# A chunkwise recurrence on TensorE: two key operands side by side in one stationary operand, one product for the turned rows of both, and the state step over 128 rows

## The reference

```python
def step(S, inp):
    r_t, w_t, k_t, v_t, kk_t, a_t = inp
    sa = jnp.einsum('bhvk,bhk->bhv', S, -kk_t)
    S = (S * w_t[:, :, None, :] + sa[..., None] * (kk_t * a_t)[:, :, None, :]
         + v_t[..., None] * k_t[:, :, None, :])
    return S, jnp.einsum('bhvk,bhk->bhv', S, r_t)
```

## Time and profile before

| | us |
|---|---|
| median of 3 executions | 2036.55 (2035.19 to 2040.31) |
| profiled execution, own time | 2034.68 |
| its span in the trace | 2032.9 |
| TensorE busy | 2001.4 |
| line 956 busy, each layer | 70.32 |
| one turn of the recurrence loop | 14.64 |

### The profile page before, as it was taken

The page is one execution under the profiler, slowest core; times in us unless marked ns, Lnnn a source line. Parts: engine busy times, 40 slices in busy tenths (PEclk is TensorE's granted clock), DMA queues, the critical chain, the costliest instruction groups (busy, mean ns, idle before and its releaser), DMA issues.

```text
span 2032.9 us, 36044 instructions
## 1 busy us (share of the span) xinstructions
PE 2001.4 (98%) x15296; PEld 1761.3 (87%) x15296; DVE 1496.4 (74%) x1311; ACT 1199.0 (59%) x1076; POOL 53.6 (3%) x36
## 2 busy tenths in 40 slices
PE   8999999999999999999999999999999999999998
PEld 6978999999998888899988888888888888888886
DVE  6656356765455766438578898888889889898896
ACT  5454453543343545445467777777777777777675
POOL 0003100000000001200000000000000000000000
PEclk9999999999999999999999999999999999999999
DMA  7432035444442322105459899898998989899895
GB/s 239 172 111 97 4 133 201 166 166 172 187 162 106 142 106 86 41 27 225 179 224 380 344 358 373 323 372 336 369 367 335 373 334 364 349 359 372 326 376 199
DMA packets 75038, 485.60 MB, mean 239 GB/s; under 512 B 13480, under 2 KB 14632, under 8 KB 17192
## 3 DMA queue, kind: packets, MB, share of 16 engines
q1 hardware_dynamic: 73816, 481.93, 61.3%
q10 hardware_dynamic: 1104, 1.92, 0.3%
HBM read 482.08 MB, written 1.74 MB: 238 GB/s over the span
## 4 chain that ended last, share of the span: by engine, by line
PE 92%; DVE 4%; ACT 2%; DMA 1%; issue 1%; POOL 0%; ACTq 0%; SPq 0%; DVEq 0%
PE PS L576 26%; PE PS L578 25%; PE PS L577 25%; PE PS L956 6%; DVE area L1910 1%; PE PS L1282 1%; PE PS L1291 1%; DVE WL L1910 1%; ACT WH L1442 1%; PE PS L914 1%; DMA ring<-in_weights 1%; PE PS L731 1%; DVE YEL L2515 0%; PE PS L1358 0%; PE PS L847 0%
## 5 line engine op out<-in xcount | busy, mean ns | idle before, releaser
L1910 DVE TENSOR_TENSOR WL<-ring,WH 128x2048 fp32r<-128x2048 f32 x410 | 934.4, 2290 | 218.0 <-ACT WH L1442 109.3
L1442 ACT ACTIVATE WH<-ring 128x2048 fp32r<-128x2048 f32 x336 | 643.1, 1916 | 158.5 <-PE PS L578 149.0
L576 PE MATMUL PS<-WH,XGH 128*128 128x512 f32 x896 | 353.7, 395 | 0.2 <-DVE XGL L1910 0.2
L578 PE MATMUL PS<-WL,XGH 128*128 128x512 f32 x896 | 349.7, 390 | 0.0
L577 PE MATMUL PS<-WH,XGL 128*128 128x512 f32 x896 | 349.1, 390 | 0.0
L578 PE MATMUL PS<-XL,WH 128*128 128x272 f32 (+1 forms) x704 | 202.5, 288 | 0.0
L1434 ACT ACTIVATE WH<-ring 128x2048 fp32r<-128x2048 f32 x74 | 141.3, 1910 | 102.0 <-PE PS L578 102.0
L578 PEld LDWEIGHTS PS<-WL,XGH 128*128 128x128 f32 x896 | 168.1, 188 | 35.8
L576 PEld LDWEIGHTS PS<-WH,XGH 128*128 128x128 f32 x896 | 168.3, 188 | 34.6 <-DVE WL L1910 0.5
L577 PEld LDWEIGHTS PS<-WH,XGL 128*128 128x128 f32 x896 | 168.4, 188 | 33.5
L576 PE MATMUL PS<-WH,HTH 128*128 128x512 f32 x448 | 176.7, 394 | 0.6
(11 more groups left out here) (350 smaller groups left out, 3432.7 us busy)
## 6 DMA issues: line engine op xcount, KB each, us to landing
ring<-in_experts SPq DMA_DIRECT2D x336, 1024.0 KB, 6.6
ring<-in_weights SPq DMA_DIRECT2D x114, 1024.0 KB, 6.9
ring<-in_weights SPq DMA_DIRECT2D x4, 576.0 KB, 4.4
ring<-in_weights SPq DMA_DIRECT2D x4, 512.0 KB, 4.0
cst<-in_consts SPq DMA_DIRECT2D x1, 1731.0 KB, 7.4
hT<-in_stream ACTq DMA_DIRECT2D x2, 544.0 KB, 7.0
out<-area SPq DMA_DIRECT2D x4, 256.0 KB, 2.0
bias_line<-lin SPq DMA_DIRECT2D x1, 672.0 KB
```

Source lines behind the costliest of these rows:

```text
L576: pe.matmul(o, lh, rh, start=first, stop=False, skip_group_check=True)
L578: return pe.matmul(o, lh, rl, start=False, stop=last, skip_group_check=True)
L1442: act.activation(WH[(BASE + j + 1) % 3][:, :], ring[b][:, 2048 * (j % 2):2048 * (j % 2) + 2048], ACT.Copy).then_inc(S("w_hi"), 1)
L1910: tt = lambda o, a_, b_, op: dve.tensor_tensor(o, a_, b_, op)
```

## The change

POOL writes AI and K of one chunk side by side into a buffer of its own (`double_keys`, four copies of 64 rows by 256, one after the other), so that they are one stationary operand of 128 columns. `products_m` multiplies it with RK in 8 matmuls on 64\*128 tiles; before these were two wide sets. `turn_rows` turns both with 8 matmuls on 64\*128 tiles and V with 8 on 64\*64; before these were three narrow sets, that of V in `products_b`. `state_step` is 8 matmuls on 128\*64 tiles instead of 16 on 64\*64. Solution and turned V now stand in one buffer UV, one in the upper and one in the lower 64 rows, so `copied_solution` becomes two ACT copies, and `copied_rows` four. DVE's `open_turned` has two half operations and stands behind `power(c - 1, 5)`; `open_rows` reads PSUM itself. `right_side` and `outputs_known` are split in a part with V and one with the state. POOL masks with four operations instead of two. In all the program has 7921 matmuls instead of 8145. Helpers that only pass an operand (`both` with `swapped`, `of_head`) and two merged semaphores are left out of the diff.

```diff
+        def doubled_keys(c):
+            home = area1[:, 8064 + 512 * c:8064 + 512 * c + 512] if c < 2 else slots_area[:, 512 * (c % 2):512 * (c % 2) + 512]
+            return home.rearrange("p (a x b) -> p a x b", a=4, x=2)
...
+                def products_m(c):
+                    cc = columns(c)
                     if c >= 2:
                         pe.wait_ge(S("r_yc"), nth(l, c - 2))
-                    both(2 + s_, 0, KK[:, :, cc], lambda r, p: AI[r, p, cc])
-                    both(2 + s_, 256, V[:, :, cc], lambda r, p: C("stack")[r, :]).then_inc(S("r_n"), 1)
-                    both(0, 0, AI[:, :, cc], lambda r, p: RK[r, :, p, cc], 2 * CH).then_inc(S("r_b"), 1)
-                def products_h(c):
-                    cc = columns(c)
-                    if c >= 2:
                         pe.wait_ge(S("r_state"), earlier(l, c - 2, lambda q: q < NCH - 1) + 1)
-                    both(1, 0, K[:, :, cc], lambda r, p: RK[r, :, p, cc], 2 * CH).then_inc(S("r_h"), 1)
+                    pe.wait_ge(S("keys_doubled"), nth(l, c))
+                    for p in range(4):
+                        for g in range(2):
+                            ins = pe.matmul(PS[:, g, 2 * CH * p:2 * CH * p + 2 * CH], doubled_keys(c)[heads[g], p, :, :].rearrange("p x b -> p (x b)"), RK[heads[g], :, p, cc],
+                                            start=True, stop=True, skip_group_check=True)
...
-                    cc = columns(c)
-                    pe.wait_ge(S("r_bc"), nth(l, c))
-                    both(0, 0, AI[:, :, cc], lambda r, p: C("stack")[r, :])
-                    both(0, 256, K[:, :, cc], lambda r, p: C("stack")[r, :]).then_inc(S("r_t"), 1)
+                    pe.wait_ge(S("r_hc"), nth(l, c))
+                    for p in range(4):
+                        for g in range(2):
+                            pe.matmul(PS[:, g, CH * p:CH * p + CH], doubled_keys(c)[heads[g], p, :, :].rearrange("p x b -> p (x b)"), C("stack")[heads[g], :],
+                                      start=True, stop=True, skip_group_check=True)
+                    for p in range(4):
+                        for g in range(2):
+                            ins = pe.matmul(PS[heads[1 - g], g, 256 + CH * p:256 + CH * p + CH], V[heads[g], p, columns(c)], C("stack")[heads[g], :],
+                                            start=True, stop=True, skip_group_check=True)
+                    ins.then_inc(S("r_t"), 1)
...
-                        both(1, 0, BHT[s_][:, 0], lambda r, p: Ust[r, p, :], first=True)
-                        both(1, 0, BHT[s_][:, 1], lambda r, p: NV[s_][r, 1, p, :], first=False).then_inc(S("r_s"), 1)
...
+                    both(1, 0, lambda g, p: BHT[s_][:, g, p, :], lambda g, p: UV[s_][:, g, p, :]).then_inc(S("r_s"), 1)
...
-                products_h(0)
-                products_b(0)
-                gate_steps(3)
+                products_n(0)
+                gate_steps(1)
+                products_m(0)
+                gate_steps(2)
                 turn_rows(0)
                 gate_steps(3)
                 level_product(0, 1)
-                pe.wait_ge(S("r_tc"), nth(l, 0))
-                products_b(1)
...
-                        products_b(c)
                         level_product(c - 1, 4)
-                        products_h(c)
+                        products_m(c)
                         level_update(c - 1, 4)
                         level_product(c - 1, 5)
-                        level_product(c, 1)
                         turn_rows(c)
                         level_update(c - 1, 5)
-                        right_side(c - 1)
+                        level_product(c, 1)
+                        right_values(c - 1)
+                    outputs_values(c - 1)
+                    if c > 1:
+                        right_state(c - 1)
                     level_update(c, 1)
                     solve(c - 1)
+                    if c > 1:
+                        outputs_state(c - 1)
                     level_product(c, 2)
                     state_step(c - 1)
+                    outputs_solved(c - 1)
                     level_update(c, 2)
-                    outputs_known(c - 1)
                     level_product(c, 3)
-                    outputs_solved(c - 1)
+                    if c + 1 < NCH:
+                        products_n(c + 1)
                     level_update(c, 3)
                 level_product(NCH - 1, 4)
-                right_side(NCH - 1)
+                right_values(NCH - 1)
                 pe.wait_ge(S("x_lo"), 5 * l + 1)
                 pe.wait_ge(S("w_lo"), g_first + 1)
...
+                def copied_m(c):
                     act.wait_ge(S("r_b"), nth(l, c))
-                    act.activation(BA[s_][:, :, :, :].rearrange("p a x b -> p (a x b)"), PS[:, 0, :], ACT.Copy).then_inc(S("r_bc"), 1)
...
-                    act.activation(BHT[s_][:, :, :, :].rearrange("p x a b -> p (x a b)"), PS[:, 0, :], ACT.Copy).then_inc(S("r_tc"), 1)
+                    for g in (1, 0):
+                        act.activation(BHT[s_][:, g, :, :], PS[:, g, 0:256].rearrange("p (a b) -> p a b", a=4), ACT.Copy)
+                        o = heads[1 - g]
+                        act.activation(UV[s_][o, g, :, :], PS[o, g, 256:512].rearrange("p (a b) -> p a b", a=4), ACT.Copy).then_inc(S("r_tc"), 1)
...
-                    act.activation(Ust[:, :, :], rows4(0), ACT.Copy).then_inc(S("r_uc"), 1)
+                    for g, o in enumerate(heads):
+                        ins = act.activation(UV[c % 2][o, g, :, :], PS[o, 1, 0:256].rearrange("p (a b) -> p a b", a=4), ACT.Copy)
+                    ins.then_inc(S("r_uc"), 1)
...
+                def double_keys(c):
+                    cc = slice(c * CH, (c + 1) * CH)
+                    o = doubled_keys(c)
+                    link(pool, pool.tensor_copy(o[0:HD, :, 0, :], AI[0:HD, :, cc]), "pool_chain")
+                    link(pool, pool.tensor_copy(o[0:HD, :, 1, :], K[0:HD, :, cc]), "pool_chain")
+                    link(pool, pool.tensor_copy(o[HD:P, :, 0, :], K[HD:P, :, cc]), "pool_chain")
+                    pool.tensor_copy(o[HD:P, :, 1, :], AI[HD:P, :, cc]).then_inc(S("keys_doubled"), 1)
+                    pool.wait_ge(S("keys_doubled"), nth(l, c))
...
+                    if n == LATE + 4:
+                        pool.wait_ge(S("g_done"), 4 * l + 4)
+                        pool.wait_ge(S("c_z"), at("c_z", l, N_UNITS[l] - 1))
+                        double_keys(0)
+                        double_keys(1)
...
-                    pool.wait_ge(S("r_bc"), nth(l, c))
-                    pool.tensor_tensor(BA[s_][:, :, 0, :], BA[s_][:, :, 0, :], bc(C("causal", 0, CH), [P, 4, CH], 1), ALU.mult)\
-                        .then_inc(S("r_bm"), 1)
+                    if c:
+                        pool.wait_ge(S("r_bm"), nth(l, c - 1))
                     pool.wait_ge(S("r_hc"), nth(l, c))
-                    pool.tensor_tensor(HA[s_][:, :, :, :], HA[s_][:, :, :, :],
-                                       bc(C("causal").rearrange("p (x b) -> p x b", x=2), [P, 4, 2, CH], 1), ALU.mult).then_inc(S("r_hm"), 1)
+                    upper, lower = BH[s_][HD:P, 0, :, 1, :], BH[s_][0:HD, 1, :, 1, :]
+                    link(pool, pool.tensor_tensor(upper, upper, bc(causal[HD:P, 1, :], [HD, 4, CH], 1), ALU.mult), "pool_chain")
+                    pool.tensor_tensor(lower, lower, bc(causal[0:HD, 1, :], [HD, 4, CH], 1), ALU.mult).then_inc(S("r_hm"), 1)
+                    pool.wait_ge(S("r_hm"), nth(l, c))
+                    for g in range(2):
+                        m = BH[s_][:, g, :, 0, :]
+                        ins = pool.tensor_tensor(m, m, bc(causal[:, 0, :], [P, 4, CH], 1), ALU.mult)
+                    ins.then_inc(S("r_bm"), 1)
+                    if c + 2 < NCH:
+                        pool.wait_ge(S("r_bm"), nth(l, c))
+                        pool.wait_ge(S("eg_done"), 8 * l + 8)
+                        pool.wait_ge(S("r_t"), nth(l, c))
+                        double_keys(c + 2)
...
-                    dve.wait_ge(S("r_bc"), nth(l, c))
-                    v(tt(TT[s_][:, :, :], BA[s_][:, :, 1, :], bc(C("turned"), [P, 4, CH], 1), ALU.mult))
+                    for g, o in enumerate((slice(0, HD), slice(HD, P))):
+                        dve.wait_ge(S(("r_bc", "r_hc")[g]), nth(l, c))
+                        ins = tt(TT[s_][o, :, :], BH[s_][o, g, :, 1, :], bc(C("turned")[o, :], [HD, 4, CH], 1), ALU.mult)
...
-                        open_rows(c)
                         power(c - 1, 4)
+                        power(c - 1, 5)
                         open_turned(c)
-                        power(c - 1, 5)
```

More of the change, by code:

```diff
@@ L950, in _, with both @@
                 heads = slice(0, HD), slice(HD, P)
-                def both(bank, col, lhs, rhs, n=CH, first=None, start=True):
+                def both(bank, col, lhs, rhs, first=None, swapped=False):
                     for p in range(4):
-                        for r in heads:
```

(40 more changed lines are left out.)

106 lines of the change are left out of this document (53 added, 53 removed).

## The result

The changed kernel takes 2043.84 us (median of 8, 2042.01 to 2045.03), the kernel before 2036.45 (median of 8): the ratio is 1.0037 with a 95% interval of 1.0028 to 1.0046, so it is slower by about 7.4 us. I had forecast 2041.5, and slower by over 0.3% with a chance of 0.35 only.

What follows compares the result with a forecast made beforehand. The recurrence itself, TensorE's streaming and ACT's and DVE's hand-overs, was taken as the bound. A turn's -1.37 + 0.96 + 1.21 gave +0.8 us; with starts and ends +5.9 in all, so 2041.5 us, range 2030 to 2047.

Steps and rivals of the forecast that it cites:

- Streaming: TensorE in a turn: 23 narrow sets and two of 0.89 us on 64*128 tiles, 1.37 us less.
- Changes of tile: Six a turn around the three new TensorE steps, where there were none: 0.16 us each, 0.96 a turn.
- Rival C: No cost between tiles that share a dimension, only the waits grow: about 2035 us; chance 0.14.
- Hand-overs: TensorE's waits in a turn for ACT, DVE and levels: 1.95 us instead of 0.74, +1.21.
- TI behind two copies: ACT's copy of TI for level_product(c - 1, 5) queues behind two copies: stall of 0.25 us becomes 0.55.
- The solution: Wait in a turn for the copied solution, now two ACT copies: 0.25 us, as before.
- `r_open_t`: Stall on DVE's open_turned, with one to two collisions with POOL's masks: 0.3 to 0.7 us a turn, 0.5 taken.
- Start: Start of each layer's recurrence: -0.45 us on TensorE; late POOL fill +0.7 in the first layer, net +0.4 in the second.
- The waits for POOL: Gate product at each layer's start waits for POOL's late fill: +0.7 us in the first layer, +1.6 in the second.
- POOL's copy: Each copy of keys by POOL takes 0.55 us, between bounds of 0.42 and 0.73; eight at the first start.
- First turn, loop and end: Per layer: first turn +0.77 us, three later turns 2.4 together, idle time before the last outputs covered, -0.35.
- The total: Both layers' recurrences: +3.1 us in the first, +2.8 in the second, together +5.9; forecast 2041.5 us.

Runs made afterwards that it cites:

- keys_twice: The changed kernel with the product of doubled keys issued twice in turns c = 2, 3, 4; 2044.0 us (one time).
- open_first: The changed kernel with DVE's open_turned(c) put back ahead of power(c - 1, 5); ratio 1.0035 to the kernel before.
- quad: The changed kernel without doubled buffer and POOL's copies; products_m and turn_rows as 16 matmuls each, interleaved over four 64*64 tiles; ratio 1.0017 to the kernel before.
- five: The kernel of four without doubled buffer and POOL's copies, with products_m and turn_rows done as in quad; ratio 0.9945 to the kernel before.
- m_64: The changed kernel with the product of doubled keys as 16 matmuls on 64*64 tiles, from the same doubled buffer; 2043.7 us (one time).
- three: The changed kernel with the edits of masks_late, rows_64 and m_first together; ratio 0.9980 to the kernel before.
- six: The kernel of five with DVE's open_turned(c) put back ahead of power(c - 1, 5); ratio 0.9948 to the kernel before.
- masks_late: The changed kernel with POOL's masks of a chunk also waiting until DVE has opened TT of that chunk; ratio 1.0027 to the kernel before.
- rows_64: The changed kernel with the turned keys as 16 matmuls on 64*64 tiles, from the same doubled buffer; ratio 1.0020 to the kernel before.
- m_first: The changed kernel with the first product of doubled keys ahead of the first gate product in each layer; ratio 1.0024 to the kernel before.
- four: The kernel of three with products_n(c + 1) moved ahead of level_product(c - 1, 5) and outputs_solved in its old place; ratio 0.9956 to the kernel before.
- pairs: The kernel of quad with each step's 16 matmuls ordered as eight on one pair of opposite tiles, then eight on the other; 2040.2 us (one time).

## Why the prediction was right, and where it was off

The mechanism and the size of a turn were right, the turn's size in part by luck, as parts that were off made up for each other. The total came 2.4 us above the forecast.

- **Streaming** (-1.37 a turn): right. The set on 64\*128 tiles is 0.89 (keys_twice).
- **Changes of tile** (0.16 each, 0.96 a turn): a little too dear, by my reading. Each change shows 0.10 us ahead of the first matmul, and the first load of 128 columns in a new mode 0.10 more (1.10 for the set ahead of its successor, less 0.89, is 0.2 in and out). I read 0.10 + 0.20 for `products_m`, 0.10 + 0.15 for the turned keys and 0.10 + 0.15 for the state step: 0.8. Rival C (nothing between tiles that share a dimension) is out.
- **Hand-overs** (1.95 a turn instead of 0.74): together with the changes of tile the sum was right (15.44 less 12.52 leaves 2.9, and I had 0.96 + 1.95), its parts weren't. TI behind two copies: 0.38 idle, 0.55 with the restart, as summed. The solution: no wait at all where I had 0.25. `r_open_t`: 0.8 idle and 1.0 with the restart, where I took 0.5, and 0.7 was my upper bound. This is the mis-sized term: I priced one to two collisions of 0.36, but three of POOL's masks lie over the three operations of DVE, and they cost 1.02 us. "SBUF — State Buffer" of the Trainium skill (who interferes with whom) calls the shared port an exclusive lock; 2.32 against 1.30 agrees.
- **Start**, up to the copy of `copied_right(0)`: +0.25 forecast and +0.2 measured in the first layer, -0.05 and +1.45 in the second. The waits for POOL were 0.58 and 1.65 us, near the 0.7 and 1.6 of the text. But behind the 1.65 us the clock fell, which I had not priced at all; that is the 1.0 us by which the second layer was worse than summed, and more. open_first has the same start without the fall: 18.47 us against 18.64 before, so -0.2, as summed.
- **POOL's copy**: 0.39 to 0.42 us, each 0.46 after the last, one of 1.5 in each layer; eight took 4.84 us at the first start (185.03 to 189.87), 0.6 each where I took 0.55.
- **First turn, loop and end** together: +0.77 + 2.4 - 0.35 = +2.8 forecast for each layer; from the copy of `copied_right(0)` to the end of the recurrence it is +2.75 in the first layer and +2.3 in the second.
- **The total**: the 6.7 us of the recurrences are read from one profiled execution of each kernel, the 7.4 us from medians. That they are close doesn't show that the rest is 0.7: outside the recurrence the same pair differs by -1.7, -0.2 and +5.3 us, in code that is the same, with the clock.

What I did not question was the alternative. I weighed one wide stationary operand against two wide sets in a row, because all rows of before had them in a row; the gain in streaming at these two steps does not need the wide operand, nor the buffer, copies and changes of tile that come with it. By itself that wasn't enough (quad is still slower than the kernel before); with the waits mended it was (five). No run puts the four tiles into the kernel before and leaves the rest of the change out, so what they are worth there isn't shown.

## What to carry to other kernels

When a step is on part of the array, ask which tiles stand empty before making its operand larger: here, sending half of the results to the other half of the partitions ran two products at once (0.97 us instead of 1.75), with no copies and no change of tile. In a chain of short steps over several engines, time saved on TensorE may count only when the wait behind it is mended too (the tiles of the turned keys gave nothing with the wait for DVE in place, and 0.18 us a turn without it); mend the wait first, then the streaming. And a late mask on POOL can cost TensorE nothing where early ones slow VectorE by a microsecond a turn.

## What was not expected of the hardware

Much of the scatter goes with the clock. Windows (10 us each) over the end of the second layer's merge, first of the kernel before, then of the changed one, whose code and order there are the same:

```profile
1010.00:1020.00 10.00, 10.00 (x90) 1.00 0.46 165
1020.00:1030.00 10.00, 9.84 (x78) 1.00 0.11 46
1030.00:1040.00 10.00, 9.77 (x52) 1.00 0.00 0
```

```profile
1010.00:1020.00 10.00, 10.00 (x86) 0.96 0.45 189
1020.00:1030.00 10.00, 10.00 (x77) 0.84 0.54 210
1030.00:1040.00 10.00, 10.00 (x40) 0.51 0.01 2
```

The part behind the recurrence took 1122.4 us in the one profile and 1127.7 in the other. 0.51 is a stretch at the lower level, 1.2 GHz. By that part the profiles fall into two groups: in open_first, m_64, three and six it took 1127.5 to 1129.4 us, as in the changed kernel, and in keys_twice, masks_late, rows_64, m_first, four, quad and pairs 1122.0 to 1124.1, as before. five is between, with 1125.6. four, five and quad have short stretches at the lower clock there (0.86 and 0.83 from 1000 to 1010 us, and 0.83 from 1010 to 1020). TensorE has one wait of 0.4 us in that part, with the fall (m_64) and without it (keys_twice), so that wait alone doesn't decide it. The kernel before alone goes from 2031 us with a mean clock of 0.997 to 2041 with 0.992. So a profile's total can't be set against another's for a few microseconds; the stretch in question can, and the medians of many runs. Why the clock falls in one execution and not in another stays open.
